# The second expert's round finishes its tokens: no final stage behind the expert rounds of a hybrid decoder step

## The reference

```
hf = rmsnorm(x, g_moe)
gsel = argmax(hf @ w_group)                        # one group of 4
top_v, top_i = top_2(logits of that group's 8 experts)
gate_w = softmax(top_v) * softmax(group logits)[gsel]
out = sum over the 2 chosen experts e of gate_w[e] * (silu(hf @ w_gate[e]) * (hf @ w_up[e])) @ w_down[e]
x = x + out
y = x * rsqrt(mean(x*x) + 1e-6) * g_final          # y_prompt (1024 rows), y_sample (64 rows)
```

## Time and profile before

| | us |
|---|---|
| median of 3 runs | 1138.63 (1138.15 to 1138.71) |
| span of the profiled execution | 1136.2 |
| what lies around the span, by the median | 2.4 |
| TensorE busy in the span | 1092.9 |
| VectorE, ScalarE, GpSimd busy | 625.3, 250.6, 80.9 |
| mean granted clock of TensorE | 0.991 |

### The profile page before, as it was taken

The page is one execution under the profiler, slowest core; times in us unless marked ns, Lnnn a source line. Parts: engine busy times, 40 slices in busy tenths (PEclk is TensorE's granted clock), DMA queues, the critical chain, the costliest instruction groups (busy, mean ns, idle before and its releaser), DMA issues.

```text
span 1136.2 us, 15240 instructions
## 1 busy us (share of the span) xinstructions
PE 1092.9 (96%) x6149; PEld 617.8 (54%) x6149; DVE 625.3 (55%) x1250; ACT 250.6 (22%) x531; POOL 80.9 (7%) x108
## 2 busy tenths in 40 slices
PE   6999999999999999999999999999899999999985
...
DMA  9109350277471002300055451016779999999968
GB/s 296 46 1 221 30 42 1 74 203 274 151 275 23 0 1 88 135 1 1 9 200 200 148 217 43 20 56 228 282 270 402 417 415 418 415 417 416 366 251 315
DMA packets 65368, 209.27 MB, mean 184 GB/s; under 512 B 13560, under 2 KB 22416, under 8 KB 57072
## 3 DMA queue, kind: packets, MB, share of 16 engines
...
q10 hardware_dynamic: 128, 0.03, 0.0%
...
## 4 chain that ended last, share of the span: by engine, by line
PE 90%; DVE 5%; issue 2%; DMA 1%; ACT 1%; ACTq 0%; SPq 0%; DVEq 0%; POOLq 0%
PE bank L713 15%; PE bank L1230 15%; PE bank L876 9%; PE bank L941 8%; PE bank L1247 7%; PE bank L1071 6%; PE bank L685 5%; PE bank L835 3%; PE bank L973 2%; PE bank L1038 2%; PE bank L1218 2%; PE bank L802 2%; PE bank L1115 1%; PE bank L983 1%; PE bank L858 1%
## 5 line engine op out<-in xcount | busy, mean ns | idle before, releaser
L713 PE MATMUL bank<-arena 128*128 128x360 f32 (+1 forms) x576 | 177.7, 468 | 1.0 <-DVE arena L1633 0.9
L1230 PE MATMUL bank<-arena 128*32 128x512 f32 x1536 | 171.7, 599 | 1.0 <-DVE arena L2349 1.0
L713 PEld LDWEIGHTS bank<-arena 128*128 128x128 f32 x576 | 108.5, 190 | 64.8 <-issue 1.5
L1230 PEld LDWEIGHTS bank<-arena 128*32 128x32 f32 x1536 | 47.7, 110 | 106.6 <-issue 105.3
L1952 DVE TENSOR_TENSOR arena<-arena,bank 128x512 f32<-128x512 f32 (+3 forms) x56 | 68.3, 1220 | 66.6 <-PE bank L941 37.5
L876 PE MATMUL bank<-arena 128*128 128x272 f32 x448 | 103.0, 392 | 0.0
L1071 PE MATMUL bank<-arena 128*128 128x512 f32 x224 | 100.6, 598 | 0.5 <-DVE arena L2117 0.5
L941 PE MATMUL bank<-arena 128*128 128x512 f32 x224 | 97.7, 593 | 0.0
L876 PEld LDWEIGHTS bank<-arena 128*128 128x128 f32 x448 | 85.0, 190 | 17.4
L2353 DVE TENSOR_TENSOR arena<-arena,bank 128x256 f32<-128x256 f32 x24 | 10.1, 420 | 150.7 <-ACT arena L1539 150.7
L1247 PE MATMUL bank<-arena 128*32 128x512 f32 x768 | 86.8, 592 | 0.6 <-ACT arena L1542 0.6
...
## 6 DMA issues: line engine op xcount, KB each, us to landing
arena<-in_w_gate SPq DMA_DIRECT2D x32, 1024.0 KB, 9.4
arena<-in_w_up SPq DMA_DIRECT2D x32, 1024.0 KB, 15.4
arena<-in_w_down SPq DMA_DIRECT2D x32, 1024.0 KB, 16.4
arena<-in_ck SPq DMA_DIRECT2D x8, 1024.0 KB, 7.2
arena<-in_cv SPq DMA_DIRECT2D x8, 1024.0 KB, 5.3
...
```

Source lines behind the costliest of these rows:

```text
L713: last = nc.tensor.matmul(b[:, 0:w], win[slot][:, k, m * P:m * P + P], ht[:, k, c0:c0 + w], start=k == 0, stop=k == KD - 1)
L1230: last = nc.tensor.matmul(bank[2 + j % 2][t0:t0 + QT, :].rearrange("p (h n) -> p h n", h=2), xgt[j % 2][:, k, t0:t0 + QT], gu[e % GUB][:, ...
```

## The change

The final stage goes, and `work_moe` with it. A slot's row is treated by its role. If the expert is the token's first, its result is stored to `work_firsts` (a DRAM table of 1088 rows, filled with x beforehand by one DMA near the middle of the program). If it is the second, then in the rounds behind it GpSimd gathers the first result (`first_rows`), the three weights of the token come from a small table in DRAM (`work_wtab`, `weights_of`), VectorE adds weight times own result to the normalized row still in `xg` (`with_own`) and weight times first result to that (`with_first`), ScalarE squares and sums (`square_z`), GpSimd raises to the power -0.5 (`root`), VectorE scales by it and g_final (`finish_rows`), and GpSimd scatters to y_prompt and y_sample (`put`, two indirect DMAs). The norm does not change if the row is scaled by the token's rstd, so the normalized row serves as the residual, and the weights and epsilon are scaled to match. The role is decided after the capacity test now, so `place` computes the swap, behind the `ro` tiles.

`xg` has four buffers for three; a buffer is free again after `with_own`. The last two slot groups (22 and 23) add straight from PSUM (`late_first`, `late_own`) and take their roots on ScalarE. Slot groups 21 to 23 hold second rows only.

```diff
-GUB, DNB, XGB = 5, 5, 3
+GUB, DNB, XGB = 5, 5, 4
+ZTB, YGB, WGB = 3, 4, 4
 # SyncE
+            sp.dma_start(firsts, I["x"]).then_inc(sem["first_in"], 16)
...
+            sp.wait_ge(sem["wt_ok"], 1)
+            sp.dma_start(wtab[0:SEQ, :].rearrange("(i p) c -> p i c", p=P), wt[:, 0:NT - 1, :]).then_inc(sem["wt_st"], 16)
...
-                if j == LATE:
...
-                    for i in ZORDER + ZREST:
-                        load_first(i, sem[FIN[i][0]])
...
-            for i in FORDER:
...
-                sp.dma_start(fy[i][0:r, :], W["moe"][TOK + i * P:TOK + i * P + r, :]).then_inc(sem[FIN[i][0]], 16)
-            for n, o in enumerate(FORDER):
-                sp.wait_ge(sem["f_out"], n + 1)
-                dst = O["y_p"][o * P:o * P + P, :] if o < 8 else O["y_s"]
-                sp.dma_start(dst, xres[0:ROWS[o], o, :]).then_inc(sem["f_st"], 16)
 # GpSimd
-            for n in range(2):
-                refetch(n)
-            for j in range(NR):
-                refetch(j + 2)
-                pool.wait_ge(sem["ya_ok"], j + 1)
-                pool.wait_ge(sem["yd_done"], j + 1)
...
-                store(j, j, f"y_st{j % 2}")
+            fetch(3, 3, "xg_in3")
+            pool.wait_ge(sem["idx_ok"], 2)
+            pool.wait_ge(sem["wt_st"], 32)
+            for c in range(WGB):
+                weights_of(c, c, f"wg_in{c}")
+            pool.wait_ge(sem["first_in"], 16)
+            for j in range(1, NR):
+                pool.wait_ge(sem["ya_ok"], j)
+                store(j - 1, j - 1, f"y_st{(j - 1) % 2}")
+                if j + 3 < NR:
+                    pool.wait_ge(sem["zt_ok"], j)
+                    fetch(j + 3, (j + 3) % XGB, f"xg_in{(j + 3) % XGB}")
+                if 3 <= j < NR - 1:
+                    root((j - 3) % WGB, (j - 3) % 4, j - 2, j - 2)
+                    pool.wait_ge(sem["pw_ok"], j - 2)
+                    weights_of(j + 1, (j + 1) % WGB, f"wg_in{(j + 1) % WGB}")
+                    pool.wait_ge(sem["o_ok"], j - 2)
+                    put(j - 3, yg[YG[j - 3]], f"o_st{(j - 3) % 4}")
+                if j - 1 < LATE:
+                    if j - 1 >= YGB:
+                        pool.wait_ge(sem[f"o_st{(j - 1) % 4}"], 32 * ((j - 1) // 4))
+                    main_first(j - 1)
+                if j == LATE:
+                    pool.wait_ge(sem["gu_full"], LATE)
+                    for c in range(LATE, NR):
+                        first_rows(c, YG[c], f"yg_in{c % 4}")
+                if j == NR - 2:
+                    for c in (NR - 4, NR - 3):
+                        root(c % WGB, c % 4, c + 1, c + 1)
+            for c in range(NR - 4, NR):
+                pool.wait_ge(sem["o_ok"], c + 1)
+                put(c, yg[YG[c]] if c < NR - 1 else zt[0], f"o_st{c % 4}")
 # ScalarE, in the rounds and behind them
-                y_first(j, "ya_ok")
+                if 2 <= j < NR - 2:
+                    square_z(j - 2)
+                if j < NR - 2:
+                    main_copy(j)
...
+            square_z(NR - 2)
+            act.wait_ge(sem["ss_ok"], NR - 1)
+            nc.scalar.activation(rsz[:, 2:3], ssz[:, 2:3], ACT.Sqrt, scale=1.0 / D, bias=wg[:, 2, 2:3]).then_inc(sem["std2_ok"], 1)
...
+            nc.scalar.activation(rsz[:, 3:4], ssz[:, 7:8], ACT.Sqrt, scale=1.0 / D, bias=ssz[:, 3:4]).then_inc(sem["std2_ok"], 1)
+            main_copy(NR - 2)
+            main_copy(NR - 1)
 # VectorE, in the rounds
+            def with_own(c):
+                dve.wait_ge(sem["ya_ok"], c + 1)
+                dve.wait_ge(sem[f"wg_in{c % WGB}"], (c // WGB + 1) * 16)
+                if c >= ZTB:
+                    dve.wait_ge(sem["ss_ok"], c - ZTB + 1)
+                V.scalar_tensor_tensor(split(zt[c % ZTB][:, :]), split(yst[c % 2][:, :]), wg[:, c % WGB, 1:2], by_column(xg[c % XGB]), MUL, ADD).then_inc(sem["zt_ok"], 1)
+
+            def with_first(c):
+                dve.wait_ge(sem[f"yg_in{c % 4}"], (c // 4 + 1) * 16)
+                dve.wait_ge(sem["zt_ok"], c + 1)
+                y = yg[YG[c]]
+                V.scalar_tensor_tensor(y[:, :], y[:, :], wg[:, c % WGB, 0:1], zt[c % ZTB][:, :], MUL, ADD).then_inc(sem["z_ok"], 1)
...
             for j in range(NR):
                 if j + 2 < NR:
                     dve.wait_ge(sem["gu_full"], j + 1)
                     main_rows(j + 2)
+                if 3 <= j < NR - 1:
+                    dve.wait_ge(sem["pw_ok"], j - 2)
+                    finish_rows(j - 3)
+                if j == NR - 2:
+                    with_first(NR - 4)
+                    with_first(NR - 3)
+                    late_first(NR - 2)
+                    late_first(NR - 1)
                 if j + 1 < NR:
                     dve.wait_ge(sem["silu_ok"], j + 2)
                     if j >= 1:
                         dve.wait_ge(sem["ht_full"], j)
                     product(j + 1, "prod_ok")
...
-                y_second(j, "yd_done")
+                if 2 <= j < NR - 2:
+                    with_first(j - 2)
+                if j < NR - 2:
+                    with_own(j)
```

407 lines of the change are left out of this document (218 added, 189 removed).

## The result

The changed kernel takes 1187.7 us (median of four runs, 1186.9 to 1189.6) against 1138.4 for the kernel before: ratio 1.043, 95% interval 1.041 to 1.045. Slower was forecast, by 16 us; it is 49 us, and above the range. The profiled execution's span is 1185.0 us (before 1136.2).

The account below looks back on a forecast made before the run. The prediction took TensorE at 11.68 us a round, with the DMA engines close behind, to bound the rounds. Rounds +26, end -10 and the rest 0 made +16 on 1138.6: 1155 us, range 1129 to 1176.

Parts of the forecast that it names:

- Routing, 0: Routing before the rounds: added small operations hidden behind VectorE's waits, 0; 1 to 2 us if that cover is gone.
- The fetch moves, +26: Expert rounds: the row fetch, issued less than a round ahead, makes TensorE's transposes wait, +26 us over 20 fetches.
- it lands after ... 10.0 in the median: Fetch in the rounds: lands 4.1 us after its start on quiet queues, 10.0 in the median, 12.3 at most.
- two rounds of three late by 1.9 us: Expert rounds: two of three fetches land 1.9 us late, 1.3 us a round on average.
- the low end of the forecast's own range for the rounds, +16: Expert rounds: smallest growth used for the forecast's own span of 1145 to 1167, +16 us.
- Part 2: The prediction's deciding step, the moved fetch in the rounds: +26 us, low end 11 or nothing, high end 38.
- Rival C, the clock: TensorE's clock in the rounds: 13 late rounds each lose a further 1.2 us, +16, 1171; chance 0.14 with rival D.
- Rival B, bytes, +11: Expert rounds: only the bytes bind, 12.2 us a round at 417 GB/s, +11, total 1140; chance 0.10.
- Rival D, the chain over two rounds: Rounds: store, gather, sum, square, copies bind at 13.9 us a round, 20 x 2.2, total 1173; 0.14 with rival C.
- The high end of 1176: Whole kernel: top of the predicted range, past rival D's total, leaving out a sum of rivals C and D.
- The end, -10: Final stage: its removal saves 10 us, from 48.1 to 37.7 counted from round 22's start; range -12 to -8.
- At no cost: Rounds: added VectorE, ScalarE and GpSimd work fits beside the 11.68 us round, GpSimd's issues taking 7.8 us, 0.

Follow-up runs that it names:

- e8: Changed kernel with the store of slot 22 moved into the overflow branch and GpSimd's last waits put behind the overflow test: 1173.0 us.
- e16: Changed kernel with a fifth fetch buffer, copies ahead of the square, gather reading normalized rows without waiting, half of w_down left out: 1146.2 us.
- e4: Kernel before with the fetch issued behind the store of four slots earlier, delayed by five GpSimd memsets to about 5.4 us into the round: 1169.4 us.
- e3: Kernel before with only the fetch moved, issued behind the store of four slots earlier, less than a round ahead of its transposes: 1157.7 us.
- e13: Changed kernel with each gate/up load issued as two halves, so packets of 4,096 bytes in place of 8,192: 1159.9 us.
- e15: Changed kernel with a fifth fetch buffer, copies ahead of the square, the reordered end of e8 and gate/up loads in 4 KB packets: 1144.6 us.
- e9: Changed kernel with a fifth fetch buffer, copies ahead of the square, and the gather reading normalized rows without waiting for the store: 1159.3 us.
- e10: Changed kernel with a fifth fetch buffer and, from the sixth expert on, only half of w_down loaded: 1162.2 us.

## Why the prediction failed, point by point

**Routing, 0, measured +3.6.** The cover that I counted on did not hold; the prediction had 1 to 2 us for that case. Two executions of the changed form without the chance shift (e8, e16) have their first transposes at 822.65 and 822.52 against 818.98. In the kernel after, the first fetch is issued 4.8 us later than before, less the shift of 2.3 it is 2.5; the other 1.1 come between fetch and transposes. Not tested by itself.

```profile
819.35 1.12 POOL L592 DMA_INDIRECT arena<-work_xn,idxg  x1 [143.24 <-DVE idxg L2339]
```

**The fetch moves, +26, measured +40.5: the step that failed.** That it would be late, in a pattern of three, and that TensorE's transposes would wait, was right. Wrong was "it lands after ... 10.0 in the median": the figure came from a queue with 288 packets a round and was carried over to one with 752, where the fetch landed after 12.8 (e4, at the same place with 288: 8.6). The prediction counted what the six transfers cost GpSimd (7.8 us of 11.68) and in bytes (0.16 MB), and not what they cost in packets. That the queues move packets one for one was readable before, at 42 a microsecond in those 5 us, where three quarters of the row packets were full rows; 752 packets are 17.7 us a round at that pace, and 12.7 at the 59 measured afterwards, both more than 11.68. The start was off too, 5.4 for 3.5, since the store took 2.24 us and not 1.0.

The pattern was wrong in its size: two rounds of three late by 1.9 us were forecast, one of three late by 4.2 to 6.8 came (and two early waits of 1.7 and 0.3). Why one was not looked into. That the position alone is worth 24.6 (e4) against the 26 forecast is in part luck: fewer waits, made up for by the clock that the sum had left out. And the low end of the forecast's own range for the rounds, +16, is not worked out anywhere; Part 2 gives 11 or nothing.

**Rival C, the clock**, was right as a term and wrong as an alternative: 10.5 us of the 40.5. Behind single waits of 4.2 to 6.8 us the next round lost 1.6 to 2.6. In e3 and e4, behind seven waits of 2.5 to 3.6 us, five lost 1.5 to 2.8 and two nothing; in e13, with waits up to 2.3, none did. So behind the forecast's 1.9 us there would probably have been no loss, and C came with the longer waits.

**Rival B, bytes, +11:** the floor is there, 11.2 in e15, where TensorE waits for weights (13.8 in e9, where it waits for none). **Rival D, the chain over two rounds,** is there as well, though smaller than the 44 us that the prediction had for it in the rounds (e10: 14.0 with part of the bytes out of the way). The prediction gave B 0.10, and C and D together 0.14, as other ways in which it could go; B and D are limits that lie under the late fetch, and come up as soon as it is mended. The high end of 1176 left out a sum of C and D. What happened was another sum, a later fetch and C: the waits and the clock behind them already fill the 40.5, and D is not seen in the kernel after: TensorE waits for nothing but the fetch there.

**The end, -10, measured +2.5.** The order (store of 22 ahead of eight puts) was right, and e8's 11.6 us show its price with the branch. Mis-sized: slot 23's product ends 16.7 us into round 22, for 11.2, because GpSimd issues four gathers and a store ahead of the root (VectorE has it at 8.7 us, for 4.3) and the two strided sums take 2.0 us and not 1.28; the last down product 4.81 us at the lower clock for 3.6; and 10.9 us behind the last put for 4.2, of which 3.3 are the branch.

**At no cost,** the added work on VectorE, ScalarE and GpSimd in the rounds: right, by e16; at the end it has a cost, as the paragraph above shows.
